# Four boundaries on 512 tokens, taken in two halves of 256 tokens with a norm chain for each half

## What is computed

```
for layer in (0, 1):
    h  = h  + 0.5 * g1  * swiglu(prenorm(h,  norm_ffn1, sh1,  sc1),  ffn1_w_in, ffn1_w_out)
    hc = hc + 0.5 * cg1 * swiglu(prenorm(hc, norm_ffn1, csh1, csc1), ffn1_w_in, ffn1_w_out)
    mix_l, mix_c = even or odd mixer of prenorm(h, norm_mix) @ w_in, prenorm(hc, norm_mix) @ w_in
    h = h + gm * (mix_l @ mix_w_out)            # layer 0: hc too
    h = h + 0.5 * g2 * swiglu(prenorm(h, norm_ffn2, sh2, sc2), ffn2_w_in, ffn2_w_out)   # layer 0: hc too

prenorm(h, gain, shift, scale) = h * rsqrt(mean(h * h) + eps) * gain * (1 + scale) + shift
swiglu(x) = (silu(x @ w_g) * (x @ w_u)) @ w_out
```

## Time and profile before

| | us |
|---|---|
| median of 3 runs | 2962.35 |
| lowest, highest | 2955.85, 2962.42 |
| the profiled execution | 2958.74 |
| its span | 2957.0 |
| TensorE busy | 2901.9 (98%) |
| VectorE busy | 1931.6 (65%) |
| ScalarE busy | 1315.2 (44%) |
| mean granted clock of TensorE | 0.997 |

### The profile page before, as it was taken

The page is one execution under the profiler, slowest core; times in us unless marked ns, Lnnn a source line. Parts: engine busy times, 40 slices in busy tenths (PEclk is TensorE's granted clock), DMA queues, the critical chain, the costliest instruction groups (busy, mean ns, idle before and its releaser), DMA issues.

```text
span 2957.0 us, 51029 instructions
## 1 busy us (share of the span) xinstructions
PE 2901.9 (98%) x19572; PEld 2561.2 (87%) x19572; DVE 1931.6 (65%) x3058; ACT 1315.2 (44%) x1952; POOL 0.2 (0%) x4
## 2 busy tenths in 40 slices
PE   9999999999999999999999999999999999999999
PEld 6888878887788878888888999999899999998998
DVE  5856763647748676334676667677776776787666
ACT  4332333423222332223335656555655555556555
POOL 0000000000000000000000000000000000000000
PEclk9999999999999999999999999999999999999999
DMA  8635642055546545332323666455456655554564
GB/s 248 199 116 176 191 128 85 30 157 157 162 138 184 167 143 150 102 94 85 114 86 97 181 177 177 135 164 171 144 148 199 177 145 155 163 168 140 162 190 139
DMA packets 614437, 439.36 MB, mean 149 GB/s; under 512 B 22172, under 2 KB 578040, under 8 KB 614136
## 3 DMA queue, kind: packets, MB, share of 16 engines
q1 hardware_dynamic: 613268, 436.70, 50.0%
q10 hardware_dynamic: 996, 0.23, 0.0%
HBM read 430.84 MB, written 1.05 MB: 146 GB/s over the span
## 4 chain that ended last, share of the span: by engine, by line
PE 88%; DVE 8%; ACT 2%; issue 1%; SPq 1%; DMA 1%; DVEq 0%; ACTq 0%
PE ps L478 27%; PE ps L479 26%; PE ps L480 26%; DVE wlo L427 2%; ACT whi L420 1%; PE ps L1838 1%; DMA raw<-ffn_w_in 1%; DVE normed L2730 1%; PE ps L1850 1%; SPq L747 1%; PE ps L895 1%; PE ps L1818 1%; DVE xl L2722 1%; PE ps L1000 0%; PE ps L1304 0%
## 5 line engine op out<-in xcount | busy, mean ns | idle before, releaser
L478 PE MATMUL ps<-xh,whi 128*128 128x256 f32 (+1 forms) x3744 | 1206.8, 322 | 23.7 <-DVE xl L2722 4.5
L479 PE MATMUL ps<-xl,whi 128*128 128x256 f32 (+1 forms) x3744 | 1185.5, 317 | 0.0
L480 PE MATMUL ps<-xh,wlo 128*128 128x256 f32 (+1 forms) x3744 | 1185.4, 317 | 0.0
L427 DVE TENSOR_TENSOR wlo<-raw,whi 128x1024 fp32r<-128x1024 f32 x732 | 868.3, 1220 | 177.5 <-ACT whi L420 174.5
L420 ACT ACTIVATE whi<-raw 128x1024 fp32r<-128x1024 f32 x731 | 747.9, 1054 | 457.7 <-PE ps L480 385.4
L478 PEld LDWEIGHTS ps<-xh,whi 128*128 128x128 f32 x3744 | 706.3, 189 | 107.0 <-issue 43.2
L480 PEld LDWEIGHTS ps<-xh,wlo 128*128 128x128 f32 x3744 | 705.3, 188 | 50.9
L479 PEld LDWEIGHTS ps<-xl,whi 128*128 128x128 f32 x3744 | 705.6, 188 | 48.2
L478 PE MATMUL ps<-hid_h,whi 128*128 128x512 f32 (+1 forms) x1056 | 353.3, 335 | 0.0
L480 PE MATMUL ps<-hid_h,wlo 128*128 128x512 f32 (+1 forms) x1056 | 351.9, 333 | 0.0
L479 PE MATMUL ps<-hid_l,whi 128*128 128x512 f32 (+1 forms) x1056 | 351.8, 333 | 0.0
(11 more groups left out here) (387 smaller groups left out, 2612.6 us busy)
## 6 DMA issues: line engine op xcount, KB each, us to landing
raw<-ffn_w_in SPq DMA_DIRECT2D x176, 512.0 KB, 5.5
mod_pair<-ada_w SPq DMA_DIRECT2D x48, 1024.0 KB, 5.3
raw<-w_in SPq DMA_DIRECT2D x96, 512.0 KB, 4.5
raw<-w_ffn_in SPq DMA_DIRECT2D x88, 512.0 KB, 4.7
raw<-w_gate SPq DMA_DIRECT2D x64, 512.0 KB, 4.0
mod_w<-ada_w SPq DMA_DIRECT2D x24, 1024.0 KB, 10.5
raw<-ffn_w_out SPq DMA_DIRECT2D x64, 384.0 KB, 4.0
raw<-ffn_w_out SPq DMA_DIRECT2D x64, 320.0 KB, 3.7
```

What stands on the lines that cost most here:

```text
L427: nc.vector.tensor_tensor(split_at(unit, wlo, s, h), raw[:, s, h, :], split_at(unit, whi, s, h).bitcast(F32), ALU.subtract).then_inc(S("lo ...
L478: nc.tensor.matmul(dst, w_h, x_h, start=start, stop=False)
L479: nc.tensor.matmul(dst, w_h, x_l, start=False, stop=False)
L480: return nc.tensor.matmul(dst, w_l, x_h, start=False, stop=stop)
```

## The change

At four boundaries, named by the stage that follows (mix: ffn1 of layer 0 to the even mixer; ffn2: its out product to ffn2; ffn1: ffn2 of layer 0 to ffn1 of layer 1; odd: ffn1 of layer 1 to the odd mixer), the last output units are done first for the tokens and then for the context. For a down part these are the last two units, for "out" the last unit (its two blocks). The sum over the first half, its root, reciprocal and spread come between the parts of the second half. The second half has its own sum, root, reciprocal and spread in the next stage: after the first unit's token half come the sum and the rows of modulation that are left (`ROWS_FIRST` gives how many are done ahead), and the spread in the middle of the second unit's token half. The first pair of the next stage (mix, ffn2, ffn1) is then four parts: unit 0 tokens, unit 1 tokens, unit 0 context, unit 1 context. In the odd stage the first two units had 256 columns already; the second sum and spread go into them. The dummy matmuls at these boundaries are gone. In the even mixer the turning of the row and VectorE's split of unit 1 move behind the pair. Some semaphores of other stages are merged into two (`small_ready`, `small_by_act`).

```diff
+HALVED = ('mix', 'ffn2', 'ffn1', 'odd')
+ROWS_FIRST = {"mix": 3, "ffn2": 5, "ffn1": 3}
...
-                    if u == 1:
+                    if u == (2 if "mix" in HALVED else 1):
...
+            def half_sum(p, added):
+
+                pe.wait_ge(S("sq_added"), added)
+                pe.wait_ge(S("root_ready"), c.of["norm"])
+                for t in range(NT * p, NT * p + NT):
+                    m = nc.tensor.matmul(ps[:, 4, t:t + 1], ss[:, t * P:(t + 1) * P], K("ones")[:, 0:1],
+                                         start=True, stop=True)
+                m.then_inc(S("ss_mm"), 1)
+
+            def half_spread(p):
+
+                pe.wait_ge(S("rstd_col"), c.of["norm"] + 1)
+                for t in range(NT * p, NT * p + NT):
+                    m = nc.tensor.matmul(ps[:, 5, t * P:(t + 1) * P], rstd_col[:, t:t + 1].to_broadcast([P, P]), ident,
+                                         start=True, stop=True)
+                m.then_inc(S("rstd_mm"), 1)
+                c.add(norm=1)
...
+            def tail_of(name, unit):
+
+                added = c.of["blocks"] + DC + CREDIT
+                c.add(blocks=DC + 2)
+                unit(added)
+                if name in MOD_AT_NORM:
+                    norm_rows(name, 0, ROWS_FIRST[name])
+                second = lambda: half_sum(1, added + 2)
+                rows = lambda: name in MOD_AT_NORM and norm_rows(name, ROWS_FIRST[name], MOD_AT_NORM[name][2])
+                return second, rows
+
...
+                def unit(added):
+                    part(0, 0)
+                    part(1, 0)
+                    part(0, 1)
+                    half_sum(0, added)
+                    part(1, 1, lambda: half_spread(0))
+                    c.units += 2
+                return tail_of(name, unit)
...
+                def unit(added):
+                    pe_blocks(pe, c, 0, 0, DC, 2 * T, xh, xl, 2, 256)
+                    pe_banks_free(pe, c, 0, 1)
+                    for h in range(2):
+                        pe_half_ready(pe, c, 0, 1, h)
+                    for b in range(2):
+                        for h in range(2):
+                            m = part(0, b, h)
+                        m.then_inc(S("half_mm"), 1)
+                    part(1, 0, 0)
+                    part(1, 0, 1)
+                    half_sum(0, added)
+                    part(1, 1, 0).then_inc(S("mm_done"), 1)
+                    half_spread(0)
+                    part(1, 1, 1).then_inc(S("mm_done"), 1)
+                    c.units += 2
+                return tail_of(name, unit)
...
+            def pair_by_halves(ready, second, rows, parts_of):
+
+                base = c.of["norm_hi"] - 2 * DC
+                def unit(s, p, among=None):
+                    cols = slice(p * T, (p + 1) * T)
+                    if p == 0:
+                        pe_banks_free(pe, c, 0, s)
+                    for k in range(DC):
+                        if p == 0:
+                            ready(s, k)
+                        if s == 0:
+                            pe.wait_ge(S("norm_lo"), base + p * DC + k + 1)
+                        for b in range(2):
+                            w_h, w_l = parts_of(s, b, k)
+                            m = three(ps[:, 2 * s + b, cols], w_h, w_l, xh[:, k, cols], xl[:, k, cols], k == 0, k == DC - 1)
+                        if among and k == DC // 2 - 1:
+                            among()
+                        if p and k % 4 == 3 and ready is by_chunks:
+                            m.then_inc(S("mm_done"), 1)
+                    if p and ready is not by_chunks:
+                        m.then_inc(S("mm_done"), 2)
+
+                unit(0, 0)
+                second()
+                rows()
+                unit(1, 0, lambda: half_spread(1))
+                unit(0, 1)
+                unit(1, 1)
...
+            def norm_by_halves(shift, name, square_part):
+
+                if name != "ffn2":
+                    act_split(act, 0, 0, c.units, (0,))
+                root_of_half(0)
+                if name != "ffn2":
+                    act_split(act, 0, 0, c.units, (1,))
+                if name != "ffn2":
+                    square_part(0, 1)
+                e0 = c.of["norm_prod"]
+                c.add(norm=1, norm_prod=2 * DC)
+                def highs(p, lo, hi):
+                    for k in range(lo, hi):
+                        act.wait_ge(S("norm_prod"), e0 + p * DC + k + 1)
+                        sl = slice(p * T, (p + 1) * T)
+                        nc.scalar.activation(xh[:, k, sl], normed[:, k, sl] if p else normed_first(name, k), ACT.Identity,
+                                             bias=shift(k, p)).then_inc(S("norm_hi"), 1)
+                highs(0, 0, 3)
+                if name == "ffn2":
+                    square_part(0, 1)
+                square_part(1, 1)
+                highs(0, 3, DC)
+                def second_root():
+                    root_of_half(1)
+                    c.add(norm=1)
+                if name == "odd":
+                    return second_root, lambda: highs(1, 0, DC)
+                act_split(act, 0, 1, c.units + 1, (0,))
+                second_root()
+                act_split(act, 0, 1, c.units + 1, (1,))
+                highs(1, 0, DC)

...
+                elif stage == "out" and args[4] in HALVED:
+                    pairs_of(act, c, 1, lambda i, s: square_unit(hT, i, s, 2, args[1]), ahead=act_split, first=True)
+                    act_split(act, 0, 1, c.units + 1)
+                    act.wait_ge(S("evac_done"), c.units + 1 + CREDIT)
+                    for b in range(2):
+                        square(hT, 4 + b, b, args[1])
+                    act_split(act, 0, 0, c.units + 2)
+                    done = c.units + 2 + CREDIT
+                    square_part = tail_squares(lambda j: act.wait_ge(S("evac_done"), done))
+                    c.units += 2
+                    c.add(blocks=DC + 2)
                 elif stage == "out":
...
+            def norm_by_halves(src, gain, shift, name, at_norm, add, squares):
...
+                def pieces(p, among={}):
+                    dve.wait_ge(S("rstd_mm"), c.of["norm"] + 1)
+                    c.add(norm=1)
+                    for k in range(DC + 2):
+                        if k < DC:
+                            product(k, p)
+                        if k >= 2:
+                            low(k - 2, p)
+                        if k in among:
+                            among[k]()
+                def add_second():
+                    if name == "ffn2":
+                        add(0, 1)
+                    add(1, 1)
+                    squares(0, 1)
+                if name != "ffn2":
+                    dve_split(dve, 0, 0, c.units, (0,))
+                    add(0, 1)
+                reciprocal(0)
+                if name != "ffn2":
+                    dve_split(dve, 0, 0, c.units, (1,))
+                pieces(0, {2: add_second, 4: lambda: squares(1, 1)})
+                if at_norm:
+                    norm_mods_copy(at_norm)
+                if name == "odd":
+                    return lambda: reciprocal(1), lambda: pieces(1)
+                dve_split(dve, 0, 1, c.units + 1, (0,))
+                reciprocal(1)
+                dve_split(dve, 0, 1, c.units + 1, (1,))
+                pieces(1)
...
+                if by_halves:
+                    context_norm[0]()
                 evacuate(0)
                 ahead(2)
-                context_norm()
+                if by_halves:
+                    context_norm[1]()
+                else:
+                    context_norm()
                 evacuate(1)
...
+                        unit_done(dve, c, 0, 0)
+                        for b in range(2):
+                            for j in range(2):
+                                sl = slice(j * T, (j + 1) * T)
+                                ins = nc.vector.scalar_tensor_tensor(
+                                    out=hT[:, 4 + b, sl], in0=ps[:, b, sl], scalar=mod[:, gate0 + 4 + b, j:j + 1],
+                                    in1=hT[:, 4 + b, sl], op0=ALU.mult, op1=ALU.add)
+                        ins.then_inc(S("evac_done"), 1)
+                        u = c.units + 1
+                        tail = tail_of(gate0, lambda j, p: ps[:, 7, j * T:(j + 1) * T] if p else ps[:, 2 + j, 0:T],
+                                       lambda j: dve.wait_ge(S("mm_done"), halves(0, u, 1) + HALF_CREDIT), lambda j: j == 1)
+                        add, squares = tail
+                        dve_split(dve, 0, 0, c.units + 2, (0,))
+                        add(0, 0)
+                        for b in range(2):
+                            sq_add(4 + b, b, args[1])
+                        dve_split(dve, 0, 0, c.units + 2, (1,))
+                        add(1, 0)
+                        squares(0, 0)
+                        squares(1, 0)
+                        c.units += 2
```

(67 more changed lines are left out.)

240 lines of the change are left out of this document (190 added, 50 removed).

## The result

| us | before | changed |
|---|---|---|
| median of 15 runs | 2960.96 | 2969.15 |
| lowest, highest | 2953.05, 2962.42 | 2960.35, 2972.11 |
| the profiled execution, its span | 2958.74, 2957.0 | 2971.95, 2970.1 |
| its mean granted clock | 0.997 | 0.992 |

The ratio is 1.0029, 95% interval 1.002 to 1.0038: a small loss, but clear of no change. The forecast was 2965 in a range of 2953 to 2975. The profiled execution of the changed kernel is one of its slowest, and none of the 15 has a lower clock (they lie between 0.992 and 0.996), so its trace shows more of the lower clock than the median run has.

A forecast was written before the change was run, and what follows sets the result against it. TensorE was taken as the bound, busy 98% of the span. Mix -2.3, ffn2 +7.1, ffn1 +0.7 and odd -3.7 sum to +1.8 us, with two clock drops +5.2; from mean 2959.8 that gives 2965, range 2953 to 2975.

The forecast's parts named there:

- four cases: Whole kernel: the forecast (chance 0.45) and three rivals, "The clock decides" (0.25), "Half of it" (0.2), "The halves hide as drawn" (0.1).
- the forecast's own range: Whole kernel: 2960 to 2969 us, the range of the main case alone, which had chance 0.45.
- Wait A: At ffn2, ahead of the first half sum: TensorE idle 6.0 us while VectorE's sums stand behind late weight splits; ends 3 and 8.
- Wait B: Before unit 1's first-token half: low weights queued behind the modulation row copy; 1.85 us at mix, 3.2 at ffn2 and ffn1.
- Cuts: All four boundaries: 516 products cut in two at 0.009 us each, together 4.6 us, range 0 to 6.
- odd: Boundary into the odd mixer: VectorE's weight split comes earlier, gain 3.7 us, ends 2.5 and 5.
- What the halves remove: Waits, fillers and short waits gone from TensorE: 5.6 us at mix, 3.4 at ffn2, 3.9 at ffn1.
- Clock: Behind the waits: two drops to 1.2 GHz at 1.7 us each, one for A, one for two 3.2 us waits: 3.4 us.
- The clock decides: Rival: five clock drops, at A, three times B and odd's first unit, 8.5 us; about 2970, slower; chance 0.25.
- Half of it: Rival: wait A at ffn2 is only 3 us and no clock drop; about 2959, no change; chance 0.2.
- The halves hide as drawn: Rival: neither wait A nor wait B comes, splits done in time; -12.5 us, about 2947, faster; chance 0.1.

The follow-up runs named there:

- the filled version: The changed kernel with dummy matmuls put where TensorE stands idle at mix, ffn2 and ffn1, every wait kept: 2964.89 us, ratio 1.0016 to the kernel before.
- the version without waits: The changed kernel with weight splits moved behind ffn2's first-half work, and reciprocal and row copy behind unit 1's splits: 2948.87 us, ratio 0.9964 to the kernel before.
- the run with wait A away: The changed kernel with both splits of the next stage's weights moved behind the first half's squares and sums at ffn2: 2959.15 us, ratio 1.0 to the kernel before.

## Why the prediction was right, and where its sizes were off

The median lies in the stated range, but that range took in three of the four cases; it is just above the forecast's own range of 2960 to 2969. What speaks for the forecast is the account by place. The waits and the chains behind them were right at all four. Without the clock, the forecast gave mix -2.3, ffn2 +7.1, ffn1 +0.7, odd -3.7, together +1.8; the filled version, in which the clock stays up, has -2.1, +6.8, +1.0 and -4.3, together +1.4.

- **Wait A**: 6.0 forecast, 5.88 measured, by the chain as drawn. The two half sums were not released sooner.
- **Wait B**: 1.85, 3.2 and 3.2 forecast, 1.77, 2.96 and 2.96 measured, behind the copy as drawn.
- **Cuts**: "One cut costs 0.009" was too low. The 0.1177 came from a down part of 256 tokens late in the kernel; the halves made here start 0.1199 apart, which makes 0.0132 a cut and 6.8 us for 516, above the upper end of 6.0 that I gave. I had the 0.1198 row and used it, for two thirds of the cuts, only for the upper end.
- **odd**: 3.7 forecast, 4.3 measured, by VectorE's chain as drawn. Its two splits were to stand 22.2 us behind the beginning of the pair, where they had stood at 26.1; they start at 21.75 (1435.22).
- **What the halves remove**: by the version without waits the boundaries are 12.3 us shorter although the cuts cost 6.8, so 19.1 is removed. I had 5.6 + 3.4 + 3.9 and a net 3.7 at odd, which with its 0.5 of cuts is 17.1. The 2 us missing here nearly cancel the 2.2 missing at the cuts; that was luck.
- **Clock**: the term that was mis-sized. "I count one drop for A and one for the two 3.2 us waits: 3.4 us." The profile has a drop at each of the four waits, two of them of double length, 8.0 us by the table; over all runs the clock takes about 6 more than before. With 6 in place of 3.4 the forecast of 2965 would have been 2967.6; the median is 2969.15. Another 1.2 of the gap is the start of the sum: the kernel before was taken as 2959.8, and its median over 15 runs is 2960.96.
- **The rivals.** "The clock decides" gave 2970 and comes nearer the median. The profiled execution bears out four of its five places, and A's drop lasts twice as long, which was its condition; none falls in odd. But a drop at each wait is not what every execution has (two traces above lack one), and its 8.5 us is above the 6 of all runs, as the forecast's 3.4 is below: the truth lies between the two. "Half of it" is out, since wait A measured 5.88. "The halves hide as drawn" is what the kernel does once the queue order is mended: -12.5 forecast for it, -12.3 in the boundaries measured. It failed here for the reason given against it.
- **What can be told apart.** "Less than 0.3% (9 us) can't be told from no change here" was too cautious: with 15 runs of each the interval is 0.2% to 0.38%.

Open: whether `whi` landing earlier would have removed wait A by itself. It wasn't tried, since the loads wait for buffers that the out units hold. Open too is why single executions differ in their stretches at 1.2 GHz, outside the boundaries and behind the same waits.

## What to carry to other kernels

When a stage is cut so that its halves overlap, go through each in-order queue and ask of every instruction between the halves what *it* waits for: here two weight splits and one small copy, none of them part of the new chain, took back all of the gain and more. Put what the critical sum needs ahead of work that waits for a load, and put a copy that waits for the last matmuls behind the splits that the next matmuls need; with these two moves the same change gains 10 us in place of losing 8. Price an idle wait of some microseconds on TensorE with the clock behind it: here 13.6 us of waits cost about 6 more on average, though not every wait and not in every execution.

## What the hardware showed that I had not expected

- Where the idle time is twice as long the stretch at 1.2 GHz is not simply longer: a wait of 5.88 and one of 2.96 us were both followed by 6.8 us, another of 2.96 (ffn1) by 3.4. In the run with ffn2 whole, the same wait of 2.97 at ffn1 was followed by none, and so was the 1.77 at mix in the run with wait A away.
- Waits are cheaper to remove than to fill: fillers kept the clock up, but 13.7 us of boundary time stayed.
